# An extra, unread bf16 product of 512 columns ahead of each tile's level products in a gated recurrence

## What is computed

```
b = jnp.cumsum(gi, axis=2)
inter = jnp.einsum('bhtk,bhkv->bhtv', qi * jnp.exp(b), S)
diff = b[:, :, :, None, :] - b[:, :, None, :, :]
decay = jnp.exp(jnp.where(causal, diff, -jnp.inf))
att = jnp.einsum('bhtk,bhtsk,bhsk->bhts', qi, decay, ki)
intra = jnp.einsum('bhts,bhsv->bhtv', att, vi)
...
S_new = jnp.exp(bC[:, :, 0, :])[..., None] * S + jnp.einsum('bhsk,bhsv->bhkv', ki * jnp.exp(bC - b), vi)
```

## Time and profile before

| | |
|---|---|
| median of 3 runs | 4579.12 us (4578.1 to 4582.39) |
| the profiled execution: time, span of its instructions | 4563.95 us, 4562.1 us |
| PE busy, share of the span | 3911.5 us, 86% |
| DVE, POOL, ACT busy | 2077.2, 1169.8, 953.1 us |
| mean granted clock of TensorE | 0.890 of full speed |

### The profile page before, as it was taken

How to read it: one execution, slowest core, us unless ns; L and a number is a source line. 1 busy time by engine, 2 the same in 40 slices (tenths; PEclk the granted TensorE clock), 3 DMA queues, 4 the chain that set the end, 5 groups by cost and what they waited for, 6 DMA issues and landing times. The chain is left out here.

```text
span 4562.1 us, 50506 instructions
## 1 busy us (share of the span) xinstructions
PE 3911.5 (86%) x19162; PEld 2697.8 (59%) x19162; DVE 2077.2 (46%) x4145; ACT 953.1 (21%) x1902; POOL 1169.8 (26%) x1039
## 2 busy tenths in 40 slices
PE   5899987769797999999568998887697979999993
PEld 3344564424366898898443446543344659889883
DVE  3699555312143333333647995563021433333335
ACT  2201134400032121121122012253001222112110
POOL 2014661222123121121230156512121232112112
PEclk8899958879897999999778998587798979999997
DMA  3111002360202111111011110024602111111101
GB/s 131 39 41 44 5 2 79 111 223 28 83 19 74 37 44 48 37 45 38 0 70 39 43 42 5 6 75 147 216 0 83 33 60 45 47 37 48 44 28 39
DMA packets 143022, 254.97 MB, mean 56 GB/s; under 512 B 24577, under 2 KB 76162, under 8 KB 142594
## 3 DMA queue, kind: packets, MB, share of 16 engines
q1 hardware_dynamic: 130562, 215.00, 13.8%
q0 software_dynamic: 12288, 37.76, 2.4%
HBM read 231.31 MB, written 21.42 MB: 55 GB/s over the span
## 5 line engine op out<-in xcount | busy, mean ns | idle before, releaser
L2300 PE MATMUL ps<-ffn_parts 128*128 128x384 f32 (+1 forms) x4608 | 777.7, 329 | 38.5 <-POOL ffn_parts L2379 38.5
L2300 PEld LDWEIGHTS ps<-ffn_parts 128*128 128x128 f32 x4608 | 773.9, 189 | 43.2 <-POOL ffn_parts L2379 38.9
L2310 PE MATMUL ps<-ffn_parts 128*128 128x512 f32 (+1 forms) x3456 | 798.6, 391 | 0.0
L2310 PEld LDWEIGHTS ps<-ffn_parts 128*128 128x128 f32 (+1 forms) x3456 | 624.3, 182 | 163.2 <-DVE arena L2431 12.0
L2431 DVE TENSOR_TENSOR arena<-arena,ps 128x1024 f32<-128x1024 f32 (+1 forms) x288 | 351.5, 1220 | 364.0 <-PE ps L2310 359.6
L889 PE MATMUL ps<-arena,arena_rest 128*128 128x512 f32 (+1 forms) x1152 | 379.2, 492 | 3.7 <-PEq L445 2.7
L899 PE MATMUL ps<-arena_rest,arena 128*128 128x512 f32 (+3 forms) x864 | 318.7, 526 | 2.3 <-ACT arena_rest L1072 2.3
L889 PEld LDWEIGHTS ps<-arena,arena_rest 128*128 128x128 f32 x1152 | 191.6, 193 | 193.4 <-issue 192.1
L2384 POOL TENSOR_TENSOR ffn_parts<-arena,ffn_parts 128x1024 fp32r<-128x1024 f32 x64 | 153.5, 2399 | 589.1 <-ACT ffn_parts L2344 589.1
L322 DVE TENSOR_SCALAR_CACHE_REDUCE arena_rest<-arena_rest,small 128x384 bf16<-128x384 f32 (+4 forms) x330 | 278.8, 876 | 2.1
L1911 PE MATMUL ps<-arena_rest,arena 128*128 128x512 f32 (+1 forms) x576 | 249.8, 593 | 1.7 <-issue 1.7
(11 more groups left out here) (282 smaller groups left out, 5112.3 us busy)
## 6 DMA issues: line engine op xcount, KB each, us to landing
arena<-in_w_down SPq DMA_DIRECT2D x32, 1024.0 KB, 7.7
arena_rest<-in_kv SPq DMA_DIRECT2D x96, 256.0 KB
arena_rest<-in_w_in SPq DMA_DIRECT2D x10, 2048.0 KB, 8.2
ffn_raw<-in_w_up SPq DMA_DIRECT2D x16, 1024.0 KB, 5.9
arena<-in_w_up SPq DMA_DIRECT2D x16, 1024.0 KB, 6.0
out_y_prompt<-arena SPq DMA_DIRECT2D x3, 4096.0 KB, 11.9
arena<-in_kv SPq DMA_DIRECT2D x32, 256.0 KB
arena<-out_y_prompt SPq DMA_DIRECT2D x2, 4096.0 KB, 29.8
```

The lines of the kernel that those rows point to most:

```text
L2300: ins = pe.matmul(bank(3 * c + b, y - x), w[:, k, :], h[:, k, x:y], start=(k == 0 and h is HH and w is WH), stop=(k == KC - 1 and w is WL))
L2310: ins = pe.matmul(bank(b0 + a)[0:R, :], u[:, c, tcol(t)], d[:, c, 512 * a:512 * a + 512], start=(c == 0 and u is UH and d is DH), stop=(c ...
```

## The change

`heads_att` issues one more product, behind the wait for PSUM and ahead of the four heads' products. It multiplies the bf16 identity with 512 columns of `start16` into the first 512 columns of the PSUM area that the tile is about to write; the heads' products write over what is needed of it, and the rest is never read.

```diff
@@ -943,6 +943,8 @@
                 if na >= 2:
                     pe.wait_ge(s_ad, na - 1)
                 cols = slice(t * P - c0, t * P - c0 + R)
+                pe.matmul(ps[:, 1024 * (na % 2):1024 * (na % 2) + 512], e["ident16"], e["start16"][:, 0:512],
+                          start=True, stop=True)
                 for h in range(4):
                     c, hh = h // 2, h % 2
                     part, a = slice(64 * hh, 64 * hh + 64), 1024 * (na % 2) + 512 * hh + 256 * c
```

## The result

The changed kernel takes 4602.30 us (median of 6 runs, 4597.21 to 4604.69) against 4580.09 for the kernel before (6 runs, 4572.55 to 4587.31): 1.0046 of its time, with a 95% interval of 1.0033 to 1.0058. It is slower by 22 us. The forecast was 54: the direction held, and the time lies in the whole range of 4592 to 4645 us, but not in the 4623 to 4645 of the main case, and the size was off by more than half.

A forecast was written before the change was run, and what follows sets the result against it. PE was taken to bound the recurrence's later groups at half clock, POOL the first; 68 products cost 49.2 us a layer, less 21.5 of pauses, rounded to 27; 4579 + 54 = 4633 us, main range 4623 to 4645, whole 4592 to 4645.

The forecast's parts named there:

- the main case: Recurrence of both layers: clock stays at 0.50, some 27 us more a layer, 4633 us, range 4623 to 4645; chance 60%.
- The price of a product: Each added 512-column product on PE at the low clock: 0.54 us from its weight load to the next load.
- The turn: PE going from a tile's 64-row products to a whole-array product: 0.25 us more for a tile following without pause.
- The sum at the low clock: 68 products a layer in the recurrence: 49.2 us of PE less 21.5 of pauses, about 27; ends 21.8 and 49.2.
- The clock stays low: 60%: PE's clock in the recurrence stays at 0.50 despite the added products, judged from busy stretches at 0.50; chance 60%.
- the second rival: Clock rises for a quarter to a third of the recurrence: +15 to +11 us a layer, 4601 to 4609 us; chance 18%.
- The first: Products lift the clock for the stage, from the second and third group's outputs: 41 us faster, 4538 us; chance 8%.
- The third: Loads and turn hidden behind running matmuls, a product costs its columns, 0.43 us: 7.5 us a layer, 4594 us; chance 9%.
- The fourth: PE's pauses in the recurrence can't be filled: 2 x 49.2 = 98 us more, 4677 us; chance 5%.
- What the profile was to show: Recurrence 27 us longer a layer at 0.50, next load after 0.54 us, PE's pauses nearly gone, POOL waiting at line 816.

The follow-up runs named there:

- e9_turns: The change's 512-column product replaced by two whole-array products of 32 columns, ahead of each tile's first and third head; +39 us, 1.0078 of the kernel before.
- e2_two: Two unread products of 512 columns ahead of each tile, where the change has one; +14 us, 1.0031 of the kernel before.
- e1_split: The change's product split into 64 columns with all 128 rows and 320 columns with 64 rows; +26 us, 1.0056 of the kernel before.
- e5_narrow: Five whole-array products of 32 columns per tile in place of the change's one of 512; +18 us, 1.0036 of the kernel before.
- e11_columns_256: The change's product with 256 columns instead of 512; +26 us, 1.0056 of the kernel before.
- e4_later_groups: The change's product only ahead of the 44 tiles of the second and third group; +22 us, 1.0055 of the kernel before.
- e12_ahead_later: Instead of the change's product, four of 512 columns per slot ahead of the wait for POOL, second and third group only; -24 us, 0.9951 of the kernel before.
- e3_first_group: The change's product only ahead of the 24 tiles of the first group; +13 us, 1.0027 of the kernel before.
- e6_ahead_of_wait: Instead of the change's product per tile, four of 512 columns per slot ahead of the wait for POOL, all groups; -12 us, 0.9974 of the kernel before.
- e7_behind_wait: Instead of the change's product per tile, four per slot behind the wait for POOL, ahead of the first tile's products; +6 us, 1.0018 of the kernel before.
- e10_both: Instead of the change's product, two per last-group tile and four per second-group slot ahead of POOL's wait; -3 us, 0.9991 of the kernel before.

## Why the prediction was right in direction and wrong in size

**The price of a product was right.** 0.54 us from load to load, forecast and measured. The turn was taken as 0.25 us; a tile in a row came to 1.59 us and not 1.65, so the turn is 1.59 - 0.855 - 0.54 = 0.20.

**The sum at the low clock held within a fifth, inside its bounds.** Three kernels that stay at 0.50 give two points: 0.44 us more per tile lengthen a layer by 10.1 and 11.0 us, 0.675 by 19.8, thus some 40 us per us of price. For the change's 1.59 - 0.855 = 0.735 that is 19.8 + 0.06 x 40 = 22.2 us a layer, an estimate, where the prediction had 27 (ends 21.8 and 49.2). Of the 4.8 us between, the turn makes 50 x 0.05 = 2.5. Two layers of 22.2 would be 4624 us, in the main case's range of 4623 to 4645: by this estimate that case would have held, had the clock stayed low.

**The step that failed is "The clock stays low: 60%".** The argument for it was that PE is busy for 7.00 of 7 us and for 9.49 of 10 at 0.50, "the nearest rows to what the changed stage will be, and I weigh them most". They weren't: those stretches held none of the new products, and PE's busy share in the profile doesn't tell the levels apart. e9_turns has PE busy for 48.05 of 50 us, with two whole-array products a tile, and stays at 0.50; the change is busy for 21.85 of 27 us at 0.99. The Trainium skill, TensorE: Matmul & The Clock Gate, Part 1, says that the low level is the default and that activity releases it. PE's busy time in the profile is not the sign of that here, and the measurement decides. Of the kernels here with a product ahead of every tile, the change and e2_two raised the clock in both layers, e1_split, e5_narrow and e9_turns not at all, and e11_columns_256 for 7 us at most; why these and not those was not measured and stays open. What the runs show in place of a clock that stays low is 34 us of full clock in each layer, and 10.6 us a layer instead of 27.

**What happened is the second rival**, given 18%: a partly lifted clock, "+15 to +11 us a layer, 4601 to 4609 us". The clock was full for 34 us of some 155 (22%, where a quarter to a third was assumed), and a layer is 10.6 us longer. That 4602 lies in the rival's span is in part luck: between its ends of +27 and -21, 22% of full clock would leave 27 - 0.22 x 48 = 16 us a layer. By the two points above, full clock gave back 22.2 - 10.6 = 12 us a layer; by e4's two layers it would be 34 x 10.7 / 20.5 = 18, and the cost at the low clock then 28 and not 22. I leave it at 12 to 18.

**The other rivals.** The first (full clock for the whole stage, 41 us faster) didn't come with this change, but e12_ahead_later, at 68 us of full clock, got over half of it. The third (a product costs its columns alone) is refuted for one product behind 64-row products, by the 0.54 us. For a second one behind it holds: 0.43 us in e2_two. A rule of the Trainium skill, TensorE: Matmul & The Clock Gate, Part 3, that a load overlaps a running product only in another group of rows (the same Part also names loads to a background weight buffer), doesn't agree with the trace there: the two whole-array loads begin at 580.16 and take 0.13 us together, and the first product runs from 580.17 on. The fourth (pauses can't be filled) is refuted by e3_first_group, whose 17 us of products a layer cost 4.9.

**What the profile was to show** came as forecast but for the clock and the pauses: POOL waits at line 816, the next load follows after 0.54 us, and everything behind the recurrence is unchanged; PE's pauses ahead of a tile's first load, said to be nearly gone, are half there: 7.3 + 6.3 us. The stretches at full clock hold 4.4 us of these 13.6, those at the low clock the rest. In e9_turns, at 0.50 throughout, 1.1 + 4.5 us of the 27.4 are left, nearer to what was forecast.

## What to carry to other kernels

Where a stage runs at half the clock and PE is the one that is waited for, cost an added product at both levels of the clock, and don't take a high busy share as proof that the level will stay. A product that does nothing can pay for itself if it lifts the clock in that stage; put it ahead of a wait in which PE stands anyway (e6_ahead_of_wait against e7_behind_wait), and only in the part that PE bounds (e12_ahead_later against e6_ahead_of_wait, 166 us a layer against 172). Time such a version in many executions: two of them scattered by 40 us.

## What was unexpected of the hardware

- Whole-array loads of the same weights one behind another cost little: two in 0.13 us, five in 0.21 (e2_two, e5_narrow), where one takes 0.10 to 0.11.
- A 64-row product of 320 columns behind a whole-array one was nearly hidden: of e1_split's 0.44 us per tile, 0.17 are the first product (575.98 - 575.81) and 0.20 the turn, which leaves 0.07, an estimate.
- The same instructions took 183.6 and 194.3 us in the two layers of one execution (e4_later_groups), 186.0 and 172.7 (e7_behind_wait), 168.7 and 184.0 (e10_both), and the difference that the trace shows is when the clock rose. The kernels that stayed at 0.50 throughout (before, e1_split, e5_narrow, e9_turns) gave both layers the same length to 0.1 us.
